# Recurrent gates as 64x64 corner blocks with an exchanged copy of their input, and the running maximum spread by four row tiles

## The reference, cut to what matters

```
# A: RG-LRU, after a causal conv4; LRU_HEADS = 8 blocks of 64 channels
xb = x.reshape(B, S, LRU_HEADS, LRU_BLOCK)
gates = einsum('bshi,ghij->gbshj', xb, w_rg).reshape(2, B, S, W) + b_rg
r, i = sigmoid(gates[0]), sigmoid(gates[1])
log_a = -LRU_C * r * softplus(-lam);  a = exp(log_a)
u = sqrt(-expm1(2 * log_a)) * (i * x)          # then h_t = a_t h_{t-1} + u_t
# C: mLSTM with a running-max stabiliser m_t per head (4 heads)
sc = exp(Dlog - m_t[..., None]) * einsum('bhctd,bhcsd->bhcts', qh, kh)
```

## Time and profile before

| | |
|---|---|
| median of the timed runs | 1416.21 us (1415.71 to 1417.16) |
| profiled execution, its own time | 1418.93 us |
| its span, first to last instruction | 1416.8 us |
| mean granted TensorE clock over the span | 0.996 |
| PE busy | 1400.2 us, 99% |
| DVE busy | 1070.9 us, 76% |
| ACT busy | 667.0 us, 47% |
| POOL busy | 57.5 us, 4% |
| DMA, all queues | 264.43 MB, mean 187 GB/s |

### The profile page before, as it was taken

One profiled execution on the slowest core, in us unless ns is written; L12 is line 12 of the kernel. 1 busy time (PEld: TensorE's weight loads), 2 busy tenths in 40 slices (PEclk: granted clock), 3 DMA queues, 4 the chain that ended last, 5 costly groups with the idle time before them and its releaser, 6 DMA issues.

```text
span 1416.8 us, 20757 instructions
## 1 busy us (share of the span) xinstructions
PE 1400.2 (99%) x8846; PEld 1255.1 (89%) x8846; DVE 1070.9 (76%) x1175; ACT 667.0 (47%) x653; POOL 57.5 (4%) x108
## 2 busy tenths in 40 slices
PE   9999999999999999999999999999999999999996
PEld 8888879999999888888878888899999998888885
DVE  5666687799888976667976666868997888766687
ACT  5444435664546444443454444347445464434441
POOL 0500000000000110000000000000000001000000
PEclk9999999999999999999999999999999999999999
DMA  8775545547644686555566555554476447656541
GB/s 277 254 228 179 182 168 171 175 149 203 197 151 160 192 242 225 193 178 179 177 209 204 198 191 180 179 179 149 151 225 178 151 149 234 204 192 204 198 150 60
DMA packets 168428, 264.43 MB, mean 187 GB/s; under 512 B 9086, under 2 KB 101584, under 8 KB 168336
## 3 DMA queue, kind: packets, MB, share of 16 engines
q1 hardware_dynamic: 163616, 249.66, 53.6%
q0 software_dynamic: 4720, 13.44, 3.3%
HBM read 260.70 MB, written 1.05 MB: 185 GB/s over the span
## 4 chain that ended last, share of the span: by engine, by line
PE 94%; DVE 4%; ACT 1%; DMA 0%; issue 0%; DVEq 0%; SPq 0%; ACTq 0%
PE ps L1439 20%; PE ps L1297 19%; PE ps L1299 18%; PE ps L1298 18%; PE ps L1441 10%; PE ps L1334 4%; PE ps L1562 2%; DVE wlo L787 1%; PE ps L1406 1%; ACT whi L553 1%; DVE big L871 1%; DVE stats L882 0%; DVE big L895 0%; DVE xtok L876 0%; DVE S L811 0%; DMA xtok<-in_x 0%
## 5 line engine op out<-in xcount | busy, mean ns | idle before, releaser
L787 DVE TENSOR_TENSOR wlo<-raw,whi 128x2048 fp32r<-128x2048 f32 x230 | 521.9, 2288 | 202.4 <-ACT whi L553 202.1
L553 ACT CAST whi<-raw 128x2048 fp32r<-128x2048 f32 x230 | 437.9, 1912 | 365.7 <-PE ps L1299 237.7
L1439 PE MATMUL ps<-xhl,whi 128*128 128x512 f32 x1280 | 446.9, 392 | 0.4 <-DVE S L802 0.2
L1441 PE MATMUL ps<-xhl,wlo 128*128 128x256 f32 x1280 | 357.9, 280 | 0.0
L1297 PE MATMUL ps<-xhl,whi 128*128 128x256 f32 x1056 | 300.3, 284 | 0.0
L1299 PE MATMUL ps<-xhl,wlo 128*128 128x256 f32 x1056 | 297.9, 282 | 0.0
L1298 PE MATMUL ps<-xhl,whi 128*128 128x256 f32 x1056 | 297.8, 282 | 0.0
L1439 PEld LDWEIGHTS ps<-xhl,whi 128*128 128x128 f32 x1280 | 240.3, 188 | 54.7 <-issue 1.4
L1441 PEld LDWEIGHTS ps<-xhl,wlo 128*128 128x128 f32 x1280 | 240.5, 188 | 1.4
L1297 PEld LDWEIGHTS ps<-xhl,whi 128*128 128x128 f32 x1056 | 200.9, 190 | 1.3 <-issue 1.0
L1298 PEld LDWEIGHTS ps<-xhl,whi 128*128 128x128 f32 x1056 | 200.8, 190 | 0.2
(11 more groups left out here) (244 smaller groups left out, 1471.5 us busy)
## 6 DMA issues: line engine op xcount, KB each, us to landing
raw<-in_ffn_w_in SPq DMA_DIRECT2D x172, 512.0 KB, 5.0
raw<-in_w_in SPq DMA_DIRECT2D x140, 512.0 KB, 4.5
raw<-in_ffn_w_out SPq DMA_DIRECT2D x88, 512.0 KB, 4.2
raw<-in_w_br SPq DMA_DIRECT2D x32, 512.0 KB, 5.1
raw<-in_w_out SPq DMA_DIRECT2D x16, 512.0 KB, 4.3
raw<-in_ple_gate_w SPq DMA_DIRECT2D x16, 512.0 KB, 4.7
gv<-in_ln_g POOLq DMA_DIRECT2D x8, 512.0 KB, 5.3
b_bc<-in_ln_b POOLq DMA_DIRECT2D x8, 512.0 KB, 6.3
```

The costliest lines, as they stand in the source:

```text
L553: nc.scalar.copy(whi[:, slot, :], raw[:, source, :]).then_inc(whi_made, 1)
L787: nc.vector.tensor_tensor(wlo[:, slot, :], raw[:, source, :], whi[:, slot, :].bitcast(F32), ALU.subtract).then_inc(wlo_made, 1)
L1439: nc.tensor.matmul(ps[:, 2 * q + u, :], w[:, k, u, P * q:P * q + P], xhl[:, :, 4 * kk + k, :], start=kk == 0 and k == 0, stop=False, skip_ ...
L1441: ins = nc.tensor.matmul(ps[:, 2 * q + u, 256:512], v[:, k, u, P * q:P * q + P], xh[:, 4 * kk + k, :], start=False, stop=kk == 1 and k == ...
```

## The change

The gate weights `wbd` become `w_gates`, 128 x 4 x 128. Tile m holds gate 0's two blocks on its diagonal and gate 1's two blocks in the other corners. For gate 1 the input half and output half lie crosswise, so its input is taken from `u_other`, a copy of `u` with the two halves of 64 partitions exchanged, which POOL makes with two DMAs of 64 partitions as soon as `u_made` is signalled. The products are 64 by 64. They move from the gap between groups 5 and 6 into group 6, between its two chunks. The running maximum is copied by ACT from partitions 0 to 3 to 32, 64 and 96, and each head's spreading product reads its own block of 32 partitions and writes its own bank. The product of head 3 shares its bank with the transposes and waits for them.

```diff
-K_ID, K_TRI, K_COS, K_SIN, K_SEL, K_ONE = 0, 128, 256, 512, 768, 1280
+K_ID, K_TRI, K_COS, K_SIN, K_SEL, K_ONE = 0, 128, 256, 512, 768, 896
@@ constants
-        c[h, K_SEL + P * h:K_SEL + P * (h + 1)] = 1.0
+        c[32 * h + h, K_SEL:K_SEL + P] = 1.0
@@ tiles
-        wbd = sb("wbd", [P, 2 * KW, P])
+        w_gates = sb("w_gates", [P, KW, P])
+        u_other = sb("u_other", [P, KW, T])
-        rows16 = sb("rows16", [16, 3, T])
-        rows, ifr = rows16[0:4], rows16[:, 0, :]
+        row_sets = sb("row_sets", [P, 3, T])
+        rows, ifr, ceilings = row_sets[0:4], row_sets[0:16, 0, :], row_sets[:, 1, :]
@@ POOL
-                    a = 64 * par
-                    pool.dma_start(
-                        wbd[a:a + 64, :, a:a + 64],
-                        w_rg[l].rearrange("g (m q) i j -> q i (g m) j", q=2)[par]).then_inc(lay_in, 16)
+                    for g in range(2):
+                        a = 64 * (par ^ g)
+                        pool.dma_start(
+                            w_gates[a:a + 64, :, 64 * par:64 * par + 64],
+                            w_rg[l].rearrange("g (m q) i j -> q g i m j", q=2)[par, g]).then_inc(lay_in, 16)
-            link(nc.gpsimd.memset(wbd[:, :, :], 0.0))
@@ POOL, after the first LayerNorm of the layer
+                            pool.wait_ge(u_made, l + 1)
+                            for a in (0, 64):
+                                pool.dma_start(u_other[a:a + 64, :, :], s4(1)[64 - a:128 - a, :, :]).then_inc(other_in, 16)
@@ ACT, ahead of the evacuation of C_Q
+                for h in range(1, 4):
+                    nc.scalar.copy(ceilings[32 * h:32 * h + 4, :], ceilings[0:4, :]).then_inc(rows_spread, 1)
@@ DVE
-                    mt = ps[:, 5 + h // 2, 256 * (h % 2):256 * (h % 2) + 256]
+                    mt = ps[:, 4 + h, 256:512]
@@ PE
-                pe.wait_ge(u_made, l + 1)
-                for g in range(2):
-                    for m in range(KW):
-                        ins = mm(ps[:, 4 + 2 * g + m // 2, 256 * (m % 2):256 * (m % 2) + 256], wbd[:, KW * g + m, :],
-                                 s4(1)[:, m, :])
-                ins.then_inc(rg_done, 1)
-                group(6)
+                def gate_blocks():
+
+                    pe.wait_ge(u_made, l + 1)
+                    pe.wait_ge(other_in, 32 * (l + 1))
+                    for m in range(KW):
+                        cols = slice(256 * (m % 2), 256 * (m % 2) + 256)
+                        for g, inputs in enumerate((s4(1), u_other)):
+                            for par in range(2):
+                                a, b = 64 * par, 64 * (par ^ g)
+                                ins = mm(ps[a:a + 64, 4 + 2 * g + m // 2, cols], w_gates[b:b + 64, m, a:a + 64],
+                                         inputs[b:b + 64, m, :])
+                    ins.then_inc(rg_done, 1)
+
+                group(6, gate_blocks)
+                pe.wait_ge(rows_spread, 3 * (l + 1))
@@ PE, the transposes and the spread
+                ins.then_inc(cols_T, 1)
                 for h in range(4):
-                    ins = mm(ps[:, 5 + h // 2, 256 * (h % 2):256 * (h % 2) + 256], kc[0:4, K_SEL + P * h:K_SEL + P * h + P],
-                             rows[:, 1, :])
+                    if h == 3:
+                        pe.wait_ge(cols_T, l + 1)
+                    ins = mm(ps[:, 4 + h, 256:512], kc[32 * h:32 * h + 4, K_SEL:K_SEL + P], ceilings[32 * h:32 * h + 4, :])
```

More of the change, by code:

```diff
@@ L310, in build @@
         rope_made = sem("rope_made")
+        other_in = sem("other_in")
+        rows_spread = sem("rows_spread")
+        cols_T = sem("cols_T")
         rot_in = sem("rot_in")
@@ L624, in _ @@
                 ffn(base + AT_FFN1, 2 * l * NFF)
-                act.wait_ge(lay_in, 96 * (l + 1))
+                act.wait_ge(lay_in, 128 * (l + 1))
                 nc.scalar.copy(wifs[:, :, 0:8], wif[:, :, :]).then_inc(wif_cast, 1)
@@ L1033, in _ @@
                 dve.wait_ge(if_done, l + 1)
-                dve.wait_ge(lay_in, 96 * (l + 1))
+                dve.wait_ge(lay_in, 128 * (l + 1))
                 ifc2 = ifc[:, :].rearrange("p (t x) -> p t x", t=TT)
@@ L1539, in _, with group @@
                           (gelu_made, l + 1), (cq_made, l + 1), (ck_made, l + 1), (co_made, l + 1)]
-                def group(g):
+                def group(g, between=None):
                     off = GROUPS[g]
@@ L1558, in group @@
                     for kk in range(2):
+                        if kk == 1 and between is not None:
+                            between()
                         cm_chunk(base + AT_IN + 2 * g + kk, kk, bank, xh, xl, first=kk == 0, last=kk == 1)
@@ L1599, in _ @@
                     nc.tensor.transpose(ps[:, 7, 4 * t:4 * t + 4], rows[:, 0, P * t:P * t + P], ident[0:4, 0:4])
-                    nc.tensor.transpose(ps[:, 7, 8 + 4 * t:12 + 4 * t], rows[:, 2, P * t:P * t + P], ident[0:4, 0:4])
+                    ins = nc.tensor.transpose(ps[:, 7, 8 + 4 * t:12 + 4 * t], rows[:, 2, P * t:P * t + P], ident[0:4, 0:4])
+                ins.then_inc(cols_T, 1)
                 for h in range(4):
-                    ins = mm(ps[:, 5 + h // 2, 256 * (h % 2):256 * (h % 2) + 256], kc[0:4, K_SEL + P * h:K_SEL + P * h + P],
-                             rows[:, 1, :])
+                    if h == 3:
+                        pe.wait_ge(cols_T, l + 1)
+                    ins = mm(ps[:, 4 + h, 256:512], kc[32 * h:32 * h + 4, K_SEL:K_SEL + P], ceilings[32 * h:32 * h + 4, :])
                 ins.then_inc(rows_T, 1)
```

## The result

The changed kernel takes 1420.20 us (median of 10 runs, 1418.27 to 1422.72); the kernel before, run beside it, 1416.47 (10 runs, 1415.71 to 1418.79). The ratio is 1.0027 with a 95% interval of 1.0018 to 1.0035: slower by 3.7 us, with an interval that does not reach 1, and a little more than the 0.2% (2.8 us) that the prediction counted as no change. The profiled execution took 1419.98 us for a span of 1417.8; before it was 1418.93 and 1416.8.

A forecast was written before the change was run, and what follows sets the result against it. TensorE, 99% busy, was taken to bound the kernel. Per layer -0.1 + 1.35 = +1.25, in all +2.5 us, gave 1418.7 or at most 1421.4; 1419.5 was taken, range 1415.6 to 1423.0.

The forecast's parts named there:

- The block of corners: Gate products on TensorE: four corners at once, 2.1 us instead of 3.46, a gain of 1.35 per layer.
- Rival (b): Gate corners go only in twos, block 3.46 + 0.4 us: +3.4 in all, 1422.9 us; chance 0.17.
- The spread: Spread of the running maximum on TensorE as row tiles: 1.35 us against 2.36, a gain of 1.0.
- The exchange: Copy of u on POOL's queue: 10.2 us available, nearest rows 7.6 to landing, costed at nothing.
- Rival (c): The exchange of u lands late; 1 us late on each layer is +2, 1421.5 us; chance 0.08.
- What is late next: Sigmoids 2.85 us later, delaying the cast and VectorE; TensorE idles 3.1 us per layer at bC_made.
- The clock: Clock falls to 1.2 GHz in or behind the bC_made wait, 7 in 10, costing 1.35 us per layer.
- +2.5, 1418.7: Sum if the timed runs before have both half-clock stretches: 1416.21 + 2.5 us.
- 1421.4: Upper sum if the timed runs before lack the half-clock stretches: 1418.93 + 2.5 us.
- My -0.1 per layer: What is left per layer of TensorE's 3.9 us gain after its waits, before the clock's cost.
- Rival (d): TensorE's gain carries through in full: 1416.21 - 7.8 = 1408.4 us; chance 0.10.

The follow-up runs named there:

- e7: The changed kernel with the block of 64x64 corners put back ahead of group 6: 1417.18 us, ratio 1.0001 to the kernel before.
- e2: The changed kernel with ScalarE's cast of the next weight chunk made before its wait for the gates: 1412.47 us, ratio 0.9965 to the kernel before.
- e9: The changed kernel with the old spread of the maximum and no ScalarE copies (gates alone): 1418.65 us, ratio 1.0015 to the kernel before.
- e1: The changed kernel with eight VectorE conv taps moved behind the product that signals bC_made: 1416.62 us, ratio 0.9998 to the kernel before.
- e3: The changed kernel with twelve unused products filling TensorE's wait for bC_made: 1418.26 us, ratio 1.0007 to the kernel before.
- e5: The kernel before with only the row-tiled spread of the maximum, ScalarE's copies included: 1413.63 us, ratio 0.9978 to the kernel before.
- e8: The changed kernel with ScalarE's cast ahead of the gates and eight conv taps behind the bC_made product: 1410.52 us, ratio 0.9955 to the kernel before.

## Why the prediction was right

**The block of corners: right.** 2.1 us predicted, 2.08 measured, four instructions at a time. Rival (b), 3.86 us and steps of two, is dead. What that says of the rule that stood beside it is in the last section.

**The spread: right.** 1.35 predicted, 1.28 measured, full clock behind it in every profile.

**The exchange: right.** The second copy was issued at about 265.8 and lands 3.4 us later at the median (the nearest rows had said 7.6), over 5 us ahead of its use; only e7, where it is used at 269.7, waits for it. Rival (c) is dead.

**What is late next: right.** Sigmoids at 276.89 (predicted 277.25), DVE idle 6.12 (6.2), bC_made at 337.84 + 1.23 = 339.07 (339.47), PE's transposes at 339.12 (339.57), 3.04 us behind the start of the last matmul, 2.76 of them idle (3.1). This execution runs 0.28 us early from 246.18 on, ahead of the change, which is most of the first and of the last two differences. One small wait was off: PE waits 0.30 us for sc_made where 0.7 was worked out. e2 shows the chain by cutting it, e9 its cause. The second path, that e1 found, I had not seen; in the changed kernel the first covers it.

**The clock: right, its share of the medians mis-sized.** The fall in or behind the new wait was given 7 in 10 and 1.35 us; between the transposes and the scores PE loses 1.45 us in layer 0 and 1.48 in layer 1, and e3 buys back 1.4 per layer. The term that was off is what the timed runs of before already paid. I left it between all of it (+2.5, 1418.7) and none (1421.4). The mean clocks say, roughly (see the experiments), about one stretch per run: (0.9975 - 0.9962) / 0.0012, with e5 as the kernel that has none. The changed kernel has (0.9975 - 0.9945) / 0.0012 = 2.5, where its one profile shows two. The difference, 1.4 stretches of 1.45 to 1.55 us, is 2.1 us. My -0.1 per layer was against a profile with half clock in it; against runs without it the same anchor costs +1.45. The mean lies between, and the medians differ by 3.7 where the two profiled executions differ by 1.05. Those were to differ by +2.5; 0.28 us ahead of the change and the faster pace of PE in layer 1, 0.9 us (last section), account for most of the rest. The 1419.5 that I took between the two ends had no number behind it, so that the median came within 0.7 us of it is partly luck; the mechanism is not.

**Rival (d)**, that the gain carries through, is what e8 makes true, at 1410.5 where 1408.4 was worked out: the gain on PE was real, and DVE's lateness, with the clock that fell for it, ate it.

## What to carry to other kernels

When the bounding engine gets shorter, look for the first place where it meets a chain of other engines with less slack than the gain, and follow that chain back to the instruction from which it is late; here it was a cast that only stood behind the gates in ScalarE's queue, and making it ahead of them, one line, gave back 7.7 us. A new idle time of some microseconds on TensorE can cost more than its length: here the clock fell with 2.76 us of idle time, and that cost 1.4 us more. And fix a chain at its root: moving work from ahead of the last signal (e1) met a second path, a buffer freed late, that began further back.

## What the runs showed of the hardware that I had not expected

**Four corners, one bank.** The corners (0,0) and (64,64) of gate 0 are different row tiles and write the same bank. The rows name neither corner nor pass, but two instructions that read `S` and two that read `u_other` start within 20 ns, at 274.87 and 274.88, and 32 instructions go in eight steps of 0.216 us, which is what one pass of 256 columns takes on the full array. I read this as one pass per corner and step, so that (0,0) and (64,64) write their bank together. The Trainium skill, TensorEngine Tiling (Array Packing), section Restrictions and Gotchas, says that different row tiles cannot access one bank at once; this trace disagrees for 64x64 tiles that write different partitions. By the same reading the first passes of all four corners start ahead of any second one, although the program has one product behind the other. The Trainium skill, TensorE: Matmul & The Clock Gate, section The mechanism, has matmuls start strictly in program order; if the two passes of a product stand side by side in PE's stream, which no row shows, that is not what happens here.

**Idle times behind which the clock fell.** Of the single waits at bC_made, the clock fell with those of 2.76 and 2.75 us (the changed kernel) and 2.69 (layer 1 of e9), and stayed up through 2.39 (layer 0 of e9), 1.99 and 1.58 (e7); it stayed up through 2.16 and 1.62 right behind it too (e1). That is no sharp line. At the turn of the layers all twelve profiles have the same two idle times of 1.3 us, their ends 5.3 us apart; the clock fell behind them in e7 and e8 and in no other. The windows, e9's three first, then e8 at the turn:

```profile
336.70:339.20 2.50, 0.20 (x2) 1.00 1.06 388
339.70:342.90 3.20, 3.20 (x30) 1.00 0.41 92
1039.80:1042.80 3.00, 3.00 (x18) 0.66 0.66 193
```

```profile
711.60:714.40 2.80, 2.69 (x10) 0.68 0.41 138
```

**Two paces at full clock.** Behind the scores the step between matmuls is 0.119 us in some executions and 0.117 in others, at a granted clock of 1.00 in both. In 25 us, layer 0 and layer 1, of e5 and then of before:

```profile
360.00:385.00 25.00, 25.00 (x216) 1.00 0.54 165
1060.00:1085.00 25.00, 25.00 (x217) 1.00 0.59 172
```

```profile
360.00:385.00 25.00, 25.00 (x214) 1.00 0.55 164
1060.00:1085.00 25.00, 25.00 (x213) 1.00 0.51 152
```

Between 350 and 438 us e5 gains 0.85 us on before by this alone, and as much in layer 1; the changed kernel gains as much in its layer 1 and nothing in layer 0. Neither the clock nor the DMA share goes with it, and its cause stays open. A difference of a microsecond between two kernels can be this.
